# Two modulation groups as GpSimd products and sums beside the projection's pairs, two others four chunks a value tile

## The reference, cut to what matters

```
cond = silu(c);  mod = cond @ w_mod + b_mod          # 2 x (6 x 2048)
h    = rmsnorm(x) * (1 + scale) + shift              # groups 0 and 1 are needed first
proj = h @ w_in + b_in                               # 640 x (88 tiles of 128 columns, and the gates)
y    = token_mix(proj);  x = x + gate1 * rmsnorm(y)  # groups 2 to 5 are needed from here on
x    = x + gate2 * rmsnorm(experts(...))
```

## Time and profile before

| | us |
|---|---|
| median of 3 runs | 3616.78 (3614.34 to 3617.36) |
| the profiled execution | 3611.75 |
| its span, first to last instruction | 3609.9 |

### The profile page before, as it was taken

How to read it: one execution, slowest core, us unless ns; L and a number is a source line. 1 busy time by engine, 2 the same in 40 slices (tenths; PEclk the granted TensorE clock), 3 DMA queues, 4 the chain that set the end, 5 groups by cost and what they waited for, 6 DMA issues and landing times. The chain is left out here.

```text
span 3609.9 us, 49885 instructions
## 1 busy us (share of the span) xinstructions
PE 3340.2 (93%) x19752; PEld 2737.6 (76%) x19752; DVE 2352.4 (65%) x2541; ACT 1778.0 (49%) x2276; POOL 332.4 (9%) x334
## 2 busy tenths in 40 slices
PE   5899999999999998999776999986999999999994
PEld 0899998888889998989656998874666666666662
DVE  1577556656555765554665334467888888888886
ACT  2444323333333334555445224444777777777774
POOL 0000000011100003223101100000010010010001
PEclk8999999999999999999988999997999999999997
DMA  9322325555654332211423434686999999999997
GB/s 414 141 92 92 109 97 186 205 199 206 205 203 163 109 114 79 60 46 35 140 58 125 167 108 140 229 307 244 382 376 398 397 376 398 397 376 397 398 375 288
DMA packets 181250, 796.75 MB, mean 221 GB/s; under 512 B 17493, under 2 KB 75093, under 8 KB 101733
## 3 DMA queue, kind: packets, MB, share of 16 engines
q1 hardware_dynamic: 163060, 702.37, 52.8%
q0 software_dynamic: 17168, 86.98, 7.2%
q10 hardware_dynamic: 864, 5.27, 0.4%
HBM read 732.10 MB, written 62.46 MB: 220 GB/s over the span
## 5 line engine op out<-in xcount | busy, mean ns | idle before, releaser
L2474 DVE TENSOR_TENSOR expert_lo<-expert_ring,first_expert_hi 128x2048 fp32r<-128x2048 f32 x288 | 660.0, 2292 | 111.7 <-ACT first_expert_hi L2411 107.8
L2411 ACT ACTIVATE first_expert_hi<-expert_ring 128x2048 fp32r<-128x2048 f32 x285 | 546.9, 1919 | 175.2 <-PE bank L2358 175.2
L2357 PE MATMUL bank<-expert_lo,xeT_hi 128*80 128x512 f32 x1024 | 402.1, 393 | 0.0
L468 PE MATMUL bank<-h_hi,part_hi 128*128 128x320 f32 x960 | 299.7, 312 | 6.1 <-DVE part_lo_b L851 3.7
L2356 PE MATMUL bank<-first_expert_hi,xeT_hi 128*80 128x512 f32 x768 | 303.4, 395 | 1.2 <-DVE xeT_lo L2479 1.2
L2358 PE MATMUL bank<-first_expert_hi,xeT_lo 128*80 128x512 f32 x768 | 299.2, 390 | 0.0
L468 PE MATMUL bank<-h_lo,part_hi 128*128 128x320 f32 x960 | 296.9, 309 | 0.0
L2474 DVE TENSOR_TENSOR expert_lo<-expert_ring,expert_hi 128x2048 fp32r<-128x2048 f32 x96 | 219.6, 2288 | 43.6 <-ACT expert_hi L2411 43.5
L675 ACT ACTIVATE part_hi<-part_x 128x1024 fp32r<-128x1024 f32 x120 | 127.4, 1061 | 242.6 <-PE bank L468 219.2
L851 DVE TENSOR_TENSOR part_lo_x<-part_x,part_hi 128x1024 fp32r<-128x1024 f32 x120 | 149.3, 1244 | 148.9 <-ACT part_hi L675 141.4
L1954 ACT ACTIVATE merge_w_hi<-merge_ring 128x2048 fp32r<-128x2048 f32 x48 | 92.0, 1916 | 288.5 <-PE bank L1863 160.0
(11 more groups left out here) (401 smaller groups left out, 7970.2 us busy)
## 6 DMA issues: line engine op xcount, KB each, us to landing
expert_ring<-d_wgate SPq DMA_DIRECT2D x128, 1024.0 KB, 7.0
expert_ring<-d_wup_e SPq DMA_DIRECT2D x128, 1024.0 KB, 7.9
expert_ring<-d_wdown SPq DMA_DIRECT2D x128, 1024.0 KB, 10.5
mod_slot<-d_wmod SPq DMA_DIRECT2D x60, 1024.0 KB, 7.4
part_b<-d_win SPq DMA_DIRECT2D x90, 512.0 KB, 3.7
front_ring<-d_wmod SPq DMA_DIRECT2D x36, 1024.0 KB, 8.2
merge_ring<-d_wout SPq DMA_DIRECT2D x32, 1024.0 KB, 4.9
front_ring<-d_win SPq DMA_DIRECT2D x29, 1024.0 KB, 5.0
```

The source lines that it names most:

```text
L468: mm = pe.matmul(part_bank[j][:, 0:HALF_T], w, a[:, kk, :], start=(kk == 0 and x == 0), stop=(kk == HALF_K - 1 and x == 2))
L2357: pe.matmul(out[0:CAP, :], a_hi, lo, start=False, stop=False)
L2411: act.activation(w_hi[n % NSPLIT][:], w[:, n % NSLOT].rearrange("p (k n) -> p k n", n=HALF), ACT.Copy).then_inc(s["we_high"], 1)
L2474: dve.tensor_tensor(w_lo[n % NSPLIT][:], w[:, n % NSLOT].rearrange("p (k n) -> p k n", n=HALF), w_hi[n % NSPLIT][:].bitcast(F32), ALU.subt ...
```

## The change

Groups 2 and 3 now come through the ring entirely: 64 chunks instead of 36, and in front of each of the weight tiles 19 to 26 the load order has four chunks; PE multiplies four chunks ahead of each of the tiles 17 to 24. The pairs hold no chunk on PE any more.

Groups 4 and 5 are cut in 256 units of 128 x 256. SP loads a unit into one of four slots (`load_unit`), nine a pair, behind the pair's part loads in its queue. GpSimd (`add_unit`) multiplies the unit by both columns of `cond` (128 x 2 x 256 results) and adds the product to an accumulator, which after 16 units holds, for each partition, a part of the sum; PE sums it over the partitions with two matmuls by a column of ones (`sum_units`, `pick`), two parts later in its order. GpSimd does the units of a pair around that pair's two stores. The gain of the gated tiles goes from GpSimd to ACT (`gate`, a second activation). The vectors are made at pair 29, turned behind the last pair, copied by DVE, and stored by SP, which waits for that store before the next phase.

```diff
-EARLY_MODS = 2 * KT + 4
+EARLY_MODS = 4 * KT
+UNIT = 256
+UNITS = D // UNIT * KT * (MOD_GROUPS - 4)
+UNIT_SLOTS = 4
+PAIR_UNITS = ((0, 1), (2,), (3,), (4,), (5, 6), (7,), (8,))
 B11, T3, T1, T2, B21, T4, B22 = range(7)
-MOD_AFTER = (B11, T1, B21)
-VECTOR_PAIR = 21
+VECTOR_PAIR = 29
...
-        if 23 <= o < 27:
-            loads.append(("mod", 2 * KT + o - 23))
+        if 19 <= o < 27:
+            loads += [("mod", 2 * KT + 4 * (o - 19) + x) for x in range(4)]
         loads.append(("win", o))
...
-        mod_slot, = overlay(mem, [("mod_slot", [P, D], F32)])
+        unit_slot = overlay(mem, [(f"mod_unit{b}", [P, UNIT], F32) for b in range(UNIT_SLOTS)])
+        scaled, acc = overlay(mem, [(n, [P, 2, UNIT], F32) for n in ("mod_scaled", "mod_acc")])
...
-        GROUP_END = {(KT * (g + 1) - EARLY_MODS - 1) // len(MOD_AFTER): g for g in range(2, MOD_GROUPS)}
+        GROUP_END = {0: 2, 2: 3, 14: 4, 28: 5}
+
+        def unit(u):
+
+            g, rest = divmod(u, D // UNIT * KT)
+            e, kk = divmod(rest, KT)
+            return g + 4, e, kk
+
+        def units_at(p, j):
+
+            return [len(PAIR_UNITS[0] + PAIR_UNITS[1] + PAIR_UNITS[2] + PAIR_UNITS[3] + PAIR_UNITS[4] + PAIR_UNITS[5]
+                        + PAIR_UNITS[6]) * p + r for r in PAIR_UNITS[j]]
...
-                def load_mod(c):
-                    if EARLY_MODS + c < N_MOD_LOADS:
-                        sp.wait_ge(s["mod_used"], EARLY_MODS + c)
-                        sp.dma_start(mod_slot[:], k.d_wmod[EARLY_MODS + c]).then_inc(s["slot_in"], 16)
+                def load_unit(u):
+                    if u < UNITS:
+                        g, e, kk = unit(u)
+                        if u >= UNIT_SLOTS:
+                            sp.wait_ge(s["unit_used"], u - UNIT_SLOTS + 1)
+                        sp.dma_start(unit_slot[u % UNIT_SLOTS][:], k.d_wmod[KT * g + kk][:, UNIT * e:UNIT * (e + 1)]
+                                     ).then_inc(unit_in[u % UNIT_SLOTS], 16)
...
-                load_mod(0)
+                loads = {B11: "b11_in", T3: "b12_in", T1: "b22_in", B21: "b21_in"}
                 for p in range(N_PAIRS):
-                    for j, sem in ((B11, "b11_in"), (T3, "b12_in"), (T1, "b22_in"), (B21, "b21_in")):
+                    for j in range(7):
                         if p + 1 < N_PAIRS:
                             sp.wait_ge(s["part_summed"], part_number(p, j) + 1)
-                            load_part(p + 1, B22 if j == T1 else j, sem)
-                        if j in MOD_AFTER:
-                            load_mod(3 * p + 1 + MOD_AFTER.index(j))
+                            if j in loads:
+                                load_part(p + 1, B22 if j == T1 else j, loads[j])
+                        for u in units_at(p, j):
+                            load_unit(u)
                 for b in range(2):
                     sp.wait_ge(s["out_made"], MADE * N_PAIRS - 1 + b)
                     sp.dma_start(k.d_proj[N_TILES - 2 + b], ob[b][:]).then_inc(k.last_stored, 16)
+                sp.wait_ge(s["vec_copied"], 1)
+                sp.dma_start(k.d_rows.rearrange("v (k p) -> (v k) p", p=P), vec_rows).then_inc(k.rows_out, 16)
+                sp.wait_ge(k.rows_out, 16)
...
+                def add_unit(u):
+                    if u < UNITS:
+                        kk, slot = unit(u)[2], u % UNIT_SLOTS
+                        both = unit_slot[slot][:].unsqueeze(1).to_broadcast([P, 2, UNIT])
+                        by = cond[:, kk, :].unsqueeze(2).to_broadcast([P, 2, UNIT])
+                        pool.wait_ge(unit_in[slot], 16 * (u // UNIT_SLOTS + 1))
+                        if kk == 0:
+                            if u > 0:
+                                pool.wait_ge(s["acc_read"], u // KT)
+                            pool.tensor_tensor(acc[:], both, by, ALU.mult)
+                            pool.drain().then_inc(s["unit_used"], 1)
+                        else:
+                            pool.tensor_tensor(scaled[:], both, by, ALU.mult)
+                            pool.drain().then_inc(s["unit_used"], 1)
+                            add = pool.tensor_tensor(acc[:], acc[:], scaled[:], ALU.add)
+                            if kk == KT - 1:
+                                add.then_inc(s["acc_made"], 1)
+                            else:
+                                pool.drain()
+
                 for n in range(N_TILES - 2):
                     p = (n - PAIR_TILE) // 2
-                    if p == VECTOR_PAIR + 3 and n % 2 == 0:
-                        pool.wait_ge(s["vec_copied"], 1)
-                        pool.dma_start(k.d_rows.rearrange("v (k p) -> (v k) p", p=P), vec_rows).then_inc(k.rows_out, 16)
+                    if n >= PAIR_TILE:
+                        for j in range(5) if n % 2 == 0 else (5,):
+                            for u in units_at(p, j):
+                                add_unit(u)
...
                     if gate_of(n):
-                        gain = k.chan[:, gate_of(n)[1]:gate_of(n)[1] + 1]
                         pool.wait_ge(s["gated_out"], n - T_Z + 1)
-                        pool.tensor_tensor(ob[n % 2][:], ob[n % 2][:], gain.to_broadcast([P, T]), ALU.mult)
-                        pool.drain()
                     pool.dma_start(k.d_proj[n], ob[n % 2][:]).then_inc(stored[n % 2], 16)
+                    if n >= PAIR_TILE and n % 2 == 1:
+                        for u in units_at(p, 6):
+                            add_unit(u)
...
-                def late_mod_chunk(c):
-                    if EARLY_MODS + c < N_MOD_LOADS:
-                        pe.wait_ge(s["slot_in"], 16 * (c + 1))
-                        mod_products(EARLY_MODS + c, mod_slot)
+                def sum_units(p, j):
+
+                    at = 7 * p + j - 2
+                    for u in units_at(*divmod(at, 7)) if at >= 0 else ():
+                        if u % KT == KT - 1 and u < UNITS:
+                            g, e, _ = unit(u)
+                            if e == 0:
+                                pe.wait_ge(s["mod_copied"], g - 1)
+                            pe.wait_ge(s["acc_made"], u // KT + 1)
+                            out = mod_sum(g)[32 * (e // 2):32 * (e // 2) + 2, UNIT * (e % 2):UNIT * (e % 2 + 1)]
+                            for c in range(2):
+                                mm = pe.matmul(out, pick[:, c, :], acc[:, c, :], start=(c == 0), stop=(c == 1))
+                            mm.then_inc(s["acc_read"], 1)
...
-                    if 21 <= o < 25:
-                        mod_chunk(2 * KT + o - 21)
+                    if 17 <= o < 25:
+                        for x in range(4):
+                            mod_chunk(2 * KT + 4 * (o - 17) + x)
...
+                pe.wait_ge(s["vec_ready"], 1)
+                pe.transpose(k.bank[4][:, 0:P], k.vec[:].rearrange("p v c k -> p (v c k)"), k.ident
+                             ).then_inc(s["vec_turned"], 1)
...
+                def gate(n):
+                    function, at = gate_of(n)
+                    act.activation(ob[n % 2][:], ob[n % 2][:], function)
+                    act.drain()
+                    act.activation(ob[n % 2][:], ob[n % 2][:], ACT.Copy, scale=k.chan[:, at:at + 1]).then_inc(s["gated_out"], 1)
...
+                dve.wait_ge(s["vec_turned"], 1)
+                dve.tensor_copy(vec_rows, k.bank[4][:, 0:P]).then_inc(s["vec_copied"], 1)
```

More of the change, by code:

```diff
@@ L210, in phase_front @@
         bias_step = sb("bias_step", [P, N_PAIRS])
+        pick = sb("pick", [P, 2, 2])
         with ExitStack() as early:
@@ L277, in phase_front @@
                                    "b11_in", "b12_in", "b21_in", "b22_in", "t_sum", "part_high", "part_low",
-                                   "part_summed", "p1_copied", "out_made", "slot_in", "gated_out")}
+                                   "part_summed", "p1_copied", "out_made", "unit_used", "acc_made", "acc_read", "gated_out")}
+        unit_in = [k.sem(f"mod_unit_in{b}") for b in range(UNIT_SLOTS)]
         k.rows_out, k.last_stored = k.sem("rows_out"), k.sem("last_stored")
@@ L359, in _ @@
                 pool.memset(rows[:], 0.0)
+                pool.memset(pick[:], 0.0)
                 pool.drain().then_inc(s["rows_zeroed"], 1)
+                for c in range(2):
+                    pool.memset(pick[:, c, c:c + 1], 1.0)
                 for kk in range(KT):
@@ L471, in part_products @@
                     mm.then_inc(s["part_summed"], 1)
+                    sum_units(p, j)
                 pe.wait_ge(s["cond_ready"], 1)
@@ L512, in _ @@
                     part_products(p, B11)
-                    late_mod_chunk(3 * p)
                     if p == 0:
@@ L523, in _ @@
                     part_products(p, T1)
-                    late_mod_chunk(3 * p + 1)
                     part_products(p, T2)
@@ L529, in _ @@
                         turn_mod(GROUP_END[p - 1])
-                    if p == VECTOR_PAIR + 1:
-                        pe.wait_ge(s["vec_ready"], 1)
```

(15 more changed lines are left out.)

## The result

The changed kernel takes 4022.61 us (median of 4 runs, 4021.11 to 4023.55) against 3616.66 for the kernel before (median of 4, 3614.34 to 3617.36): 1.1123 times as long, 95% interval 1.1104 to 1.1143. The forecast was 3925, the range 3770 to 4040. The span went from 3609.9 to 4021.3, 411.4 us more, and it splits at two points: the first product of the pairs starts at 683.25 (before 552.88, +130.4), and the fetch that follows the pairs starts at 1799.32 (before 1386.3), so the pair stage takes 1116.1 us (+282.7). What follows took 2222.0 us, 1.6 less than before.

What follows compares the result with a forecast made beforehand. PE's queue was taken to bound both stages. The profiled 3611.75 + 120 (value tiles) + 184 (pairs) + 3 (end) = 3919, forecast as 3925 us since the median is 5 higher; own range 3810 to 4020, over all 3770 to 4040.

Steps and rivals of the forecast that it cites:

- The likeliest case: Value tiles +120 us by a load without cover, pairs +184 by GpSimd's serial queue: 3925 us, chance 0.78.
- rival 1: Pairs: GpSimd keeps up, its period below PE's 24.75 us; 3669 us in all, chance 0.07.
- rival 2: Pairs: GpSimd's sums and drains cost more, 43 us a pair; 4170 us in all, chance 0.11.
- rival 3: Both stages: PE's matmul count alone sets the end, the fourth chunk's load in time; 3582 us, chance 0.04.
- the period: Pairs: GpSimd's serial time for one pair, 25.1 + 9.35 = 34.4 us, said to pace PE.
- the 3 us priced for the end: Behind the last pair: vectors turned and stored there instead of beside pair 24, one DMA and a copy, +3 us.
- The late issue: Value tiles: SP issues the fourth chunk's load only 7.77 us after PE ends the tile before.
- the clock's price: Value tiles: after idling, PE runs at a lower granted clock, about 1.5 us lost a tile.
- the two stores: Pairs: GpSimd's two stores with the drain ahead of each, (0.65 - 0.18 + 0.58) x 2 = 2.1 us a pair.
- The lock: Pairs: GpSimd and DVE's two-SBUF-tile operations shut each other out; 0.85 x 11 = 9.35 us a pair, bounds 0 and 12.
- First unit: Start of the pair stage: the first unit is there 7.5 us in, after B11 of pair 0 and a small load.
- The path by GpSimd's stores: Pairs: stores stand behind GpSimd's units, ACT waits for them before writing out_rows, and PE waits for that before B21.

Runs made afterwards that it cites:

- The memset run: The changed kernel with every product and sum of GpSimd replaced by a memset of 1024 elements, which reads nothing from SBUF: 3747.66 us.

## Why the prediction was right, and where its sizes were off

**The likeliest case held**: both stages became longer by the two mechanisms named, a load without cover in the value tiles and GpSimd's serial queue in the pairs. GpSimd didn't keep up (rival 1), it wasn't as slow as 43 us a pair (rival 2), and PE's matmul count didn't set the end (rival 3). The time lies in the range over all, 3770 to 4040, but 3 us over the forecast's own 3810 to 4020, because the period of 37.5 is over its 37. By spans the sum was 104 us short: 10 in the value tiles and 96 in the pair stage, into which the 3 us priced for the end went; what follows took 1.6 less.

**The value tiles, 120 predicted, 130 measured.** The late issue (7.77 predicted, 7.87 seen) and PE's wait (13.07 less 2.76 for three chunks is 10.3; 10.37 and 10.56 seen) were right. Short was the clock's price: at a granted clock of 0.50 the fourth chunk took 1.89 us instead of 1.04, and the products 15.9 (417.4 to 433.3) instead of 14.08 + 1.5. The mean tile came to 130.4 + 4.7 = 135.1 over eight, 16.9 above its 14.08, so 31.0 instead of 29.7.

**The period, 34.4 predicted, 37.5 measured, is the term that was mis-sized**, 89 of the 104 us. From the groups above, over 256/9 = 28.44 pairs:

| us a pair | predicted | measured | worked out |
|---|---|---|---|
| products | 9.2 | 9.4 | 256 x 1.04 |
| sums | 10.1 | 10.8 | 240 x 1.28 |
| lost to DVE | 9.35 | 6.8 | 766.3 of busy time less the two rows above |
| drains | 3.2 | 2.6 | 240 x 0.18, and 29.7 ahead of products |
| drains behind a store, excess | none | 3.35 | 138.5 less 240 x 0.18 |
| stores | 2.1 | 2.5 | 32.6 + 38.3 |
| accumulator | 0.45 | 1.0 | 28.0 |
| unit loads | none | 1.2 | 33.8 |

The step that failed is the one of the two stores: it priced the drain ahead of a DMA and the DMA itself, and not the drain of the operation that comes next. That one lasts 1.0 to 4.0 us instead of 0.18; moving the stores to SyncE removed the excess whole. The rows priced too low or at nothing come to 6.4 us a pair, those priced too high to 3.2, so that the forecast came this near is in part luck. The lock above all was taken too high, and this hid part of the miss. Its price was near: in the kernel with SyncE's stores, where GpSimd has few gaps, it is (815.8 - 573.4)/28.44 = 8.5 us a pair. But I let all 11 DVE operations of a pair meet GpSimd, and in the changed kernel GpSimd spends (268.3 + 32.6)/28.44 = 10.6 us of a pair in drains, waits and stores (the idle times and the stores of its groups), where they pass free. Unit loads I took as always early enough; SP issues them in one queue with the part loads, and 14 came late.

The Trainium skill (SBUF — State Buffer, Who interferes with whom) lets a Vector instruction with two SBUF inputs contend with a GpSimd instruction that reads SBUF and not with one that only writes. The memset run agrees on both sides (0.95 us a memset, 1226 ns a split). From the 2.6 cycles an element of the Trainium skill's GPSIMD Engine Reference (Elementwise — side-by-side cycle accounting) the prediction estimated 1.11 us for either operation; the trace differs, 1.04 for the product and 1.28 for the sum, and the measurement decides. No run here shows why the two differ.

**The ends of the pair stage.** First unit: 9.5 us in, predicted 7.5. Behind the last sum: 39.7 us, predicted 31.8 + 3, with the vectors' store in it. PE's longest waits were for the accumulators, 190.0 us, and for DVE's low parts, 88.8; the part loads and B21, which I had named, do not stand among them. The path by GpSimd's stores is there all the same, but it reaches PE another way than by B21. Waits of ACT over the pair stage, and timelines of ACT, DVE and PE behind the store at 988.27:

```profile
ACT out_rows L769 <- DMA d_proj<-out_rows: 149.2, 18, 14.1
```
```profile
993.18 0.53 ACT L769 ACTIVATE out_rows<-bank,chan 128x320 f32<-128x320 f32 x1 [4.99 <-DMA d_proj<-out_rows]
...
995.14 1.04 ACT L734 ACTIVATE part_hi<-part_x 128x1024 fp32r<-128x1024 f32 x1
996.21 2.33 DVE L916 TENSOR_TENSOR part_lo_x<-part_x,part_hi 128x1024 fp32r<-128x1024 f32 x1 [5.19 <-ACT part_hi L734]
998.60 0.63 PE L526 MATMUL bank<-s_hi,part_hi 128*128 128x320 f32 x1 [3.68 <-DVE part_lo_x L916]
```

ACT waits for the store, its high parts stand behind that wait in its queue, DVE's low part waits for the high part, and PE for the low part. With SyncE's stores the same wait of ACT is 12.2 us, and PE's for low parts 39.1.

## What to carry to other kernels

Before work is moved into a ring's order, follow each slot's release: a load that is let go behind the products of the tile before must be used behind the products of its own tile, or the whole of it is idle time (10.1 us a tile here in the mean, gone when one line was moved). GpSimd, which here both computes and issues DMAs, paid for the DMA again at its next drain, so the price of an operation added there is to be read behind a DMA too. And two-input work on GpSimd stretches VectorE's two-input operations: the version in which GpSimd only sums, and is far from being the bound, has PE wait 33.1 us for low parts and is 9.6 us slower than the one that leaves the 32 chunks on PE.

## What the runs showed of the hardware that was not expected

- A drain right behind GpSimd's first operation after a DMA that it issued lasted 1.0 to 4.0 us instead of 0.18. It did so with memsets in the place of the reading operations as well (1.1 to 4.0, once 0.5), and the excess is gone when SyncE issues the DMA. What GpSimd does in that time, no run shows.
- Removing idle time from GpSimd raised the lock's loss from 193 to 242 us over the stage: of 167 us taken out of its queue, 49.5 came back as longer operations.
- A block of four chunks behind a tile's products costs 0.94 us a chunk, less than the 1.17 of one chunk ahead of a tile and the 1.40 in a pair.
